# FFN gate and up products by Strassen's scheme, weight sums made by accumulating transfers

## The chip, the core and the metric

The kernel runs on one core of a Trainium2 chip, in one launch. The metric is the device time of the launch in microseconds. Engines: PE multiplies, ACT and DVE work elementwise, POOL helps and issues some of the transfers, SP issues the others.

## What is computed

A hybrid block (gated linear attention and a state space scan, then a gated FFN) on 1024 tokens of width 1024 with 256 context tokens, followed by two attention layers. The FFN is what the change touches:

```python
def swiglu(h, w_gate, w_up, w_down):
    return (jax.nn.silu(h @ w_gate) * (h @ w_up)) @ w_down

x_lat = x_lat + m_lat[2][:, None] * rms_norm(y_lat, norm_mix_post[layer])
f_lat = swiglu(modulate(rms_norm(x_lat, norm_ffn_pre[layer]), m_lat[3], m_lat[4]),
               w_gate[layer], w_up[layer], w_down[layer])
x_lat = x_lat + m_lat[5][:, None] * rms_norm(f_lat, norm_ffn_post[layer])
```

with `w_gate` and `w_up` of 1024 x 2816 and `w_down` of 2816 x 1024, in float32.

## The kernel before, in words

Activations lie with features on partitions and tokens along the free axis; "half" `ch` is one of two blocks of 512 tokens. Each float32 product is made of three products of a narrower type: every weight and every activation is split into a high half and a low half, and `pe_gemm` (L350) issues high x high, high x low and low x high for each block of 128 rows.

Weights go through one stream, class `Weights` (L251). A unit is up to 128 x 1024 elements per partition block: SP loads it into one of three `stage` slots (`sp_weights`, L302), ACT casts it to its high half `whi` (`act_weights`, L319), DVE subtracts to get the low half `wlo` (`dve_weights`, L332), PE uses both; there are four slots of halves. Each engine runs through its own program in order and calls its weight function two units ahead of the product it is at. All orders are written by hand.

The stages, with their places in the profile's time: modulation and projections; the scans (some 415 to 700 us: state space first, `pool_ssd` L1464, then gated linear attention, `pool_gla` L1917); the output product `wo` with the norms around it (`pe_out` L2312, `act_out`, `dve_out`, `pool_out` L2338; second token half from about 713 us); the FFN (`pe_ffn` L2377, `act_ffn`, `dve_ffn`, 764 to 1512 us); the two layers.

Small steps of norms, additions and splits run beside the products: class `Beside` (L2133) holds a list, and each `tick()` pops one step on every engine. `OUT1` holds the steps beside the second half of `wo`, `FFN0` and `FFN1` those beside the FFN of each token half. `Halves` (L2095) is the split of the FFN's input: for each 128 features one ACT step (add the shift, round to the high half) and one DVE step (low half). PE starts on the first 128 features once they are split.

FFN: the hidden width is cut in `PARTS` of 8, 8 and 6 blocks of 128. In a part, each block takes a gate product and an up product (24 matmuls of 512 columns each), ACT's Silu, DVE's multiplication, ACT's high half `uh` and DVE's low half `ul`; then eight down products add to the output `yc`.

POOL issues the loads of `x` (`xc`, one token half at a time, here from `pool_out` and `pool_moves` L2474) and stores. DVE's scale step of the post norm waits for the load of `x` together with the norm.

The functions that the diff touches, as the profile numbers them:

Of the kernel before, what the change touches and what calls it, by code (L numbers as in the profile page):

```python
# [4 lines left out]
ALU = mybir.AluOpType  # L5
# [10 lines left out]
NTB = 9  # L16
# [16 lines left out]

def down_units():
    return [(k, n, c, 128) for k, n in ((0, 8), (8, 8), (16, 6)) for c in range(0, 1024, 128)]
# [6 lines left out]
    "wg": fm(1024, 0, DFF),  # L42
    "wu": fm(1024, 0, DFF),
# [82 lines left out]
class Engine:  # L126
# [81 lines left out]
    def dma_start(self, out, in_):  # L208
        return IssuedDma(self.e and self.e.dma_start(out, in_))
# [41 lines left out]
class Weights:  # L251
# [4 lines left out]

    def __init__(self, S, H, L, land, hi, lo, aps):
        self.S, self.H, self.L, self.land, self.hi, self.lo, self.aps = S, H, L, land, hi, lo, aps
        self.seq, self.half, self.by, self.last, self.count = [], [], {}, {}, 0
        self.rows = None  # L260
        self.restart()
# [4 lines left out]
    def take(self, key, name, i, raw, count, *step):  # L266
        u = self.u
        self.u += 1
        if u == len(self.seq):
            self.seq.append((name, i, raw))  # L270
            self.half.append(self.count)
            self.count += not raw
# [3 lines left out]
        return u  # L276

# [4 lines left out]
    def staged(self, u):  # L282
        k, nk, c, n = self.shape(u)
        return self.S[:, u % self.NS, 0:nk * n]

    def halves(self, u):
        k, nk, c, n = self.shape(u)
        return [x[:, self.half[u] % self.NH, 0:nk * n] for x in (self.H, self.L)]
# [5 lines left out]
    def half_before(self, u):  # L294

        for v in range(u - 1, -1, -1):
            if not self.seq[v][2] and self.half[v] == self.half[u] - self.NH:
                return v
        return None


def sp_weights(e, W, upto):  # L302
    while W.sp_u <= min(upto, len(W.seq) - 1):
# [5 lines left out]
        if u >= W.NS:  # L309
            v = u - W.NS  # L310
            if W.seq[v][2]:
                e.wait_ge(*W.used(v))
            else:
                e.wait_ge(*W.lo[v])
        e.dma_start(W.staged(u), W.aps[name][off:off + 128 * nk * n].rearrange("(p x) -> p x", p=128)).then_inc(
            *W.land[u % W.NS].up(u, by=16))


def act_weights(e, W, upto):  # L319
    while W.hi_u <= min(upto, len(W.seq) - 1):  # L320
# [4 lines left out]
        e.wait_ge(*W.land[u % W.NS][u])  # L325
        v = W.half_before(u)
        if v is not None:
# [4 lines left out]
def dve_weights(e, W, upto):  # L332

    while W.lo_u <= min(upto, len(W.seq) - 1):
# [7 lines left out]
        v = W.half_before(u)  # L342
        if v is not None:
            e.wait_ge(*W.used(v))
        e.wait_ge(*W.land[u % W.NS][u])
# [4 lines left out]
def pe_gemm(e, W, bank, psum, key, name, units, rhs, nch, N, done, count, M=128, among=range(8), each=False, cuts=None):  # L350
# [5 lines left out]
    for n, i in enumerate(units):  # L356
# [5 lines left out]
        for ka, kb in zip(cuts or (0, nk), (cuts or (0, nk))[1:]):  # L362
            for ci, (b, free) in enumerate(bs):
# [19 lines left out]
                if n == len(units) - 1:  # L383
                    done.mark(key, ci)
                    if each and ci == nch - 1:
                        done.mark("row", key, nk - 1)

# [25 lines left out]
def mixer(K):  # L413
# [20 lines left out]
    stage = K.W.S[:, :, :].rearrange("p a b -> p (a b)")  # L434
# [168 lines left out]
    def dve_mod_row(e, m, D, ctx):  # L603
# [3 lines left out]
        e.wait_ge(*W.land[u % W.NS][u])  # L607
# [855 lines left out]

    def pool_ssd(e):  # L1464
# [667 lines left out]

class Beside:  # L2133
# [14 lines left out]
def blocks(K):  # L2148
# [30 lines left out]
    xc, nx, gg, sqf = v(3, 8, 512), (v(8, 8, 512), v(7, 8, 512)), v(8, 2, 512), v(8, 4, 512, off=1024)  # L2179
    yc = (v(1, 8, 512), v(2, 8, 512))  # L2180
    fh, fl, uh, ul = (v(i, 8, 512, dt=F32R) for i in (4, 0, 5, 6))
    w0 = v(1, 8, HT)
# [9 lines left out]
    def residual(key, st, ch, col, dst, sq4, ready, free, by_two=None):  # L2192
        n = Norm((key, ch), st, yc[ch], 512, aff[:, col, :], yc[ch], sq4, rs2[:, 0:512], ready, free=free, by_two=by_two)
# [14 lines left out]
    def last_of(st, key):  # L2208
# [3 lines left out]
                       [(sout.dve, ("lo", "f0", 7)), (sout.act, ("hi", "f0", 7))] if ch else [(K.sgla.pe, ("yo", 7))],  # L2212
                       (lambda k: [(sout.act, (("wo", 0, 2 * k + 1), 0))]) if ch == 0 else None) for ch in range(2)]
# [3 lines left out]
                  by_two=pair_of(sout, ("post", ch)), late=[(sout.act, ("sq", ("pre", ch), 3))])  # L2217
             for ch in range(2)]
    hf = [Halves(f"f{ch}", sout, fh, fl, nx[ch], lambda k, ch=ch: [(sout.dve, ("sc", ("pre", ch), k))],
                 [(sout.pe, (("wo", 0, 7), 0))] if ch == 0 else [(sffn.pe, (("wu", 0, 21), 0))],  # L2220
                 B=mod[:, 24:32]) for ch in range(2)]
    DOWN = [[(sffn.dve, (("wd", ch, 2, 7), 0))] for ch in range(2)]
    n_end0 = residual("end", sffn, 0, 4, xc, sqf, [*DOWN[0], (xld, ("r", 0))],
                      [(sout.pe, ("root", ("pre", 1), 0))])
# [1493 lines left out]
```

## Time and profile before

| | |
|---|---|
| median of three runs | 3363.24 us (3360.55 to 3364.39) |
| the profiled execution's own time | 3361.19 us |
| its span, first to last instruction | 3359.4 us |
| mean granted TensorE clock | 0.988 of full |
| PE, DVE, ACT, POOL busy | 97%, 49%, 39%, 8% of the span |
| bytes moved | 328 MB, 98 GB/s over the span |

Durations of matmuls overlap in the profile, so what one costs is read from the distance of starts. A window's DMA share is the mean busy share of the 16 DMA engines in it, and can stand slightly over 1 by rounding at its edges. A transfer's issue on an engine is short; its landing comes later.

### The profile page before, as it was taken

The page shows a single profiled execution, that of the slowest core. Times are in us where ns is not written, and L with a number is a line of the kernel's source. Part 1 is how long each engine was busy: PE and PEld are TensorE (multiplying, and loading weights), DVE is VectorE, ACT ScalarE, POOL GpSimd, SP SyncE. Part 2 cuts the span into 40 slices and gives each one's busy share as a digit, 9 for nine tenths or more (in the row PEclk, how much of TensorE's full clock was granted, in tenths as well). Part 3 has the DMA queues.
Part 4 walks back from the last instruction along what each step waited for, and adds up shares of the span by engine and source line. Part 5 has one row for each costly group of instructions (what it writes and reads, how often), then busy time and mean ns, then how long its engine had stood idle before and what let it go on. Part 6 is the DMA issues. An engine that isn't in the chain of part 4 may idle for free.

```text
span 3359.4 us, 43733 instructions
## 1 busy us (share of the span) xinstructions
PE 3256.7 (97%) x18179; PEld 2585.9 (77%) x18179; DVE 1660.1 (49%) x2404; ACT 1321.2 (39%) x2266; POOL 252.8 (8%) x302
## 2 busy tenths in 40 slices
PE   6899888899999999999999999999999999999999
PEld 6677656787878878889955579999999555688887
DVE  6767576554343443345454553444434545534433
ACT  4532455454232333234445543333334455423322
POOL 1000313400000000000120000000000300000001
PEclk8999989999999999999999999999999999999999
DMA  6545213133333334333200112442432001124323
GB/s 246 167 156 164 82 44 114 58 127 112 120 115 96 97 94 170 94 94 118 88 1 7 51 48 89 132 131 85 149 128 85 6 7 51 47 88 134 108 94 113
DMA packets 97749, 328.24 MB, mean 98 GB/s; under 512 B 11456, under 2 KB 12880, under 8 KB 96784
## 3 DMA queue, kind: packets, MB, share of 16 engines
q1 hardware_dynamic: 77120, 252.55, 23.5%
q0 software_dynamic: 18896, 68.63, 5.9%
q10 hardware_dynamic: 1536, 4.26, 0.3%
q8 instruction: 144, 2.36, 0.3%
q14 instruction: 53, 0.43, 0.0%
HBM read 299.19 MB, written 26.21 MB: 97 GB/s over the span
## 4 chain that ended last, share of the span: by engine, by line
PE 90%; DVE 5%; ACT 2%; DMA 1%; issue 1%; ACTq 0%; DVEq 0%; POOL 0%; POOLq 0%
PE psum L146 88%; DVE mixer L175 2%; PE psum L149 2%; DVE mixer L185 1%; DVE wlo L175 1%; DMA mixer<-in_wm 1%; DVE junk L189 1%; DMA stage<-in_wi 0%; ACT whi L163 0%; DMA hold<-in_wq 0%; ACT arena L154 0%; ACT mixer L154 0%; ACT mixer L155 0%; DVE mixer L180 0%; ACT mixer L163 0%
## 5 line engine op out<-in xcount | busy, mean ns | idle before, releaser
L146 PE MATMUL psum<-region,whi 128*128 128x260 f32 (+2 forms) x7616 | 1831.6, 333 | 1.8 <-DVE region L185 1.8
L146 PEld LDWEIGHTS psum<-region,whi 128*128 128x128 f32 (+1 forms) x7616 | 1279.7, 186 | 164.5 <-DVE region L185 3.1
L146 PE MATMUL psum<-region,wlo 128*128 128x260 f32 (+2 forms) x3808 | 1265.8, 332 | 0.0
L175 DVE TENSOR_TENSOR wlo<-stage,whi 128x1024 fp32r<-128x1024 f32 (+2 forms) x454 | 510.3, 1126 | 677.3 <-ACT whi L163 676.6
L146 PEld LDWEIGHTS psum<-region,wlo 128*128 128x128 f32 (+1 forms) x3808 | 711.2, 187 | 78.4
L163 ACT CAST whi<-stage 128x1024 fp32r<-128x1024 f32 (+2 forms) x454 | 432.2, 968 | 214.2 <-PE psum L146 173.4
L154 ACT ACTIVATE arena<-psum 128x512 f32<-128x512 f32 (+2 forms) x412 | 193.2, 469 | 775.1 <-PE psum L146 771.9
L146 PE MATMUL psum<-arena 128*128 128x512 f32 (+11 forms) x1072 | 382.6, 480 | 1.9 <-ACT arena L154 1.4
L163 ACT COPY arena<-psum 128x260 f32<-128x260 f32 (+9 forms) x345 | 151.5, 444 | 402.4 <-PE psum L146 395.5
L175 DVE TENSOR_TENSOR arena<-arena,psum 128x512 f32<-128x512 f32 (+1 forms) x220 | 125.7, 572 | 327.3 <-PE psum L146 326.9
L175 DVE TENSOR_TENSOR arena<-arena 128x512 f32<-128x512 f32 (+8 forms) x341 | 204.5, 617 | 152.6 <-ACT arena L154 146.3
L146 PEld LDWEIGHTS psum<-arena 128*128 128x128 f32 (+5 forms) x1072 | 166.8, 182 | 129.6 <-issue 102.7
L163 ACT CAST region<-arena 128x512 fp32r<-128x512 f32 (+3 forms) x202 | 120.4, 616 | 228.7 <-DVE arena L175 215.6
L146 PE MATMUL psum<-mixer 64*64 64x64 f32 (+8 forms) x1876 | 184.7, 292 | 23.1 <-DVE mixer L175 14.3
L198 DVE TENSOR_REDUCE arena<-psum 128x1 f32<-128x264 f32 (+8 forms) x225 | 107.1, 505 | 199.4 <-PE psum L146 199.4
L146 PEld LDWEIGHTS psum<-mixer 64*64 64x64 f32 (+3 forms) x1876 | 129.9, 168 | 82.7 <-issue 34.3
L175 DVE TENSOR_TENSOR region<-arena,region 128x512 fp32r<-128x512 f32 (+2 forms) x188 | 117.8, 646 | 56.2 <-ACT region L163 54.0
L146 PE MATMUL psum<-hold,arena 128*128 128x384 f32 (+1 forms) x432 | 142.5, 486 | 2.4 <-DMA hold<-in_wq 2.4
L146 PEld LDWEIGHTS psum<-hold,arena 128*128 128x128 f32 (+1 forms) x432 | 77.5, 180 | 68.7 <-issue 14.9
L175 DVE TENSOR_TENSOR mixer<-mixer 128x512 f32<-128x512 f32 (+3 forms) x104 | 102.8, 999 | 36.9 <-ACT mixer L154 18.4
L146 PE MATMUL psum<-hh,whi 128*128 128x512 f32 (+3 forms) x240 | 91.7, 382 | 19.3 <-DVE hl L175 8.4
L154 ACT ACTIVATE arena<-arena 128x1040 f32<-128x1040 f32 (+7 forms) x111 | 97.0, 882 | 29.5 <-DVE arena L175 27.2
(166 smaller groups left out, 2677.6 us busy)
## 6 DMA issues: line engine op xcount, KB each, us to landing
stage<-in_w SPq DMA_DIRECT2D x144, 512.0 KB, 3.4
stage<-in_wi SPq DMA_DIRECT2D x55, 512.0 KB, 4.4
stage<-in_wo SPq DMA_DIRECT2D x48, 512.0 KB, 3.5
stage<-in_wg SPq DMA_DIRECT2D x44, 512.0 KB, 3.5
stage<-in_wu SPq DMA_DIRECT2D x44, 512.0 KB, 3.5
stage<-in_wm SPq DMA_DIRECT2D x42, 512.0 KB, 3.6
stage<-in_wd SPq DMA_DIRECT2D x32, 512.0 KB, 3.5
arena<-xr_scratch POOLq DMA_DIRECT2D x5, 2080.0 KB, 9.4
```

Source lines behind the costliest of these rows:

```text
L146: return Issued(self, self.e and self.e.matmul(out, w, x, start=start, stop=stop, skip_group_check=True))
L149: return Issued(self, self.e and self.e.transpose(out, a, ident))
L154: return Issued(self, e and e.activation(out, a, func, scale=scale))
L163: return Issued(self, e and e.copy(out, a))
L175: return Issued(self, e and e.tensor_tensor(out, a, b, op))
L185: return Issued(self, e and e.scalar_tensor_tensor(out, a, s, b, op0, op1))
L189: return Issued(self, e and e.tensor_tensor_reduce(out=out, in0=a, in1=b, scale=1.0, scalar=0.0, op0=ALU.mult, op1=ALU.add, accum_out=total))
L198: return Issued(self, e and e.tensor_reduce(out, a, AX.X, op, negate=negate))
```

## The change

Two neighbouring blocks of 128 hidden columns, the two halves of the 1024 input features and the two halves of a token block form a 2 x 2 by 2 x 2 block product. It is computed with seven products of 512 features x 128 columns x 256 tokens instead of eight (`PRODUCTS`). With a11, a12, a22 and a21 the quarters of the input (the first index counts tokens), the products use a11, a12, a22 and the sums s1 to s4 of quarters, and weight blocks 11, 22, 21 and the sums T1 to T4 of blocks.

- Weights: units of gate and up are now quarters (128 x 512 per unit), the stream's slots may be taken in halves, and two more weight tensors `tg` and `tu` hold T1 to T4.
- `tg` and `tu` are scratch tensors in device memory. POOL issues eight plain copies of blocks of `wg` and `wu` into them at the start of the scans (`weight_copies`), six accumulating transfers at the end of `pool_ssd` (`weight_sums(e, 0)`, behind a wait for the copies) and four at the start of `pool_out` (`weight_sums(e, 1)`, behind a wait for the six). SP's first load from either waits for the last of these.
- Input: `Quarters` replaces `Halves`. ACT adds the shift to all eight pieces in place, then eleven steps make the sums on DVE and the high and low halves of seven operands.
- Results: of a group's four PSUM banks three hold two products in turn. ACT copies M1, M5 and M7 out, DVE forms C11 to C22 with additions of 256 columns. Gate and up of a pair then take the old path, 1024 wide.
- `PARTS` counts pairs: 4, 4, 3. Buffers in the arena are laid out anew; the load of the first tokens' residual and of the positions is moved in POOL's order.

```diff
+PRODUCTS = (("M1", "11", "a11", "a"), ("M5", "T1", "s1", "c"), ("M7", "T3", "s3", "d"), ("M6", "T2", "s2", "b"),
+            ("M3", "22", "s4", "c"), ("M2", "21", "a12", "a"), ("M4", "T4", "a22", "d"))
+KEPT = {"M1": "m1", "M5": "m5", "M7": "m7"}
+BLOCKS = {"11": (0, 0), "T1": (0, 1), "T3": (1, 1), "T2": (2, 1), "22": (2, 0), "21": (3, 0), "T4": (3, 1)}
+def pe_pair(e, W, bank, psum, key, name, j, h, done, A, leave, tick):
+    us = W.pair(key, name, j, done)
...
+        e.wait_ge(*h(x))
+        e.wait_ge(*W.hi[u])
+        e.wait_ge(*W.lo[u])
+        for k in range(kt):
+            e.matmul(o, wh[:, k, :], h.hi[x][:, k, :], b not in begun and k == 0, False)
+            e.matmul(o, wh[:, k, :], h.lo[x][:, k, :], False, False)
+            ins = e.matmul(o, wl[:, k, :], h.hi[x][:, k, :], False, k == kt - 1)
...
+    def weight_copies(e):
+        for name, t in (("wg", "tg"), ("wu", "tu")):
+            for to, of in ((0, 0), (1, 1), (2, 2), (3, 3)):
+                e.dma_start(block_of(t, to), block_of(name, of)).then_inc(*K.tcopy.up(t, to, by=16))
+    def weight_sums(e, step):
+        e.wait_ge(*(K.tsum[0]["tu", 3] if step else K.tcopy["tu", 3]))
+        for name, t in (("wg", "tg"), ("wu", "tu")):
+            for to, of, b in ((2, t, 0), (3, t, 0)) if step else ((0, name, 1), (1, name, 2), (3, name, 2)):
+                e.dma_start(block_of(t, to), block_of(of, b), accum_op=ALU.add).then_inc(*K.tsum[step].up(t, to, by=16))
...
         pool_intervals(e)
+        weight_copies(e)
...
+        weight_sums(e, 0)
         G.mark("end")
...
+class Quarters:
+    ACT_ORDER = ("a11", "a22", "a12", "s1", "s3", None, None, "s2", None, None, "s4")
+    DVE_ORDER = (("lo", "a11"), ("lo", "a22"), ("sum", "s1"), ("sum", "s3"), ("lo", "a12"), ("lo", "s1"), ("sum", "s2"),
+                 ("lo", "s3"), ("lo", "s2"), ("sum", "s4"), ("lo", "s4"))
...
     def pool_out(e, bs):
+        K.weight_sums(e, 1)
         e.wait_ge(*K.sgla.pe["turn", 7])
         e.dma_start(xc, XT[:, :, 0:512]).then_inc(*xld.up("x", 0, by=16))
...
-    PARTS = ((0, 8), (8, 8), (16, 6))
+    PARTS = ((0, 4), (4, 4), (8, 3))
...
+            K.W.need[t] = (K.tsum[1], ("tu", 3))
```

**Order on POOL, the end of the scans.** `mixer` and `hold` are SBUF buffers of the scans, `arena` that of the later stages, `y_scratch` a tensor in device memory. Before:

```order
L175 TENSOR_TENSOR mixer<-mixer,hold 128x512
L209 DMA y_scratch<-mixer 128x4x128 x4
L175 TENSOR_TENSOR mixer<-mixer 128x512 x11
...
L171 COPY mixer<-hold 64x2x4x64 x2
L209 DMA arena<-in_xT 128x8x512
```

Now:

```order
L182 TENSOR_TENSOR mixer<-mixer,hold 128x512
L218 DMA y_scratch<-mixer 128x4x128 x4
L217 DMA tg_scratch<-in_wg 352x2048 x3
L217 DMA tu_scratch<-in_wu 352x2048 x3
L182 TENSOR_TENSOR mixer<-mixer 128x512 x11
...
L178 COPY mixer<-hold 64x2x4x64 x2
L217 DMA tg_scratch<-tg_scratch 352x2048 x2
L217 DMA tu_scratch<-tu_scratch 352x2048 x2
L218 DMA arena<-in_xT 128x8x512
```

Six accumulating transfers stand between the last store of the first scan and the first operation of the second, four before the load of x.

**Order on DVE, the start of the FFN.** `region` holds the operands of products, `arena` the values they are made from. Before:

```order
L185 SCALAR_TENSOR_TENSOR region<-arena,mod,region 128x512
L185 SCALAR_TENSOR_TENSOR arena<-arena,aff 128x512
L185 SCALAR_TENSOR_TENSOR region<-arena,mod,region 128x512 x4
L175 TENSOR_TENSOR wlo<-stage,whi 128x1024 x2
L175 TENSOR_TENSOR arena<-arena,psum 128x512
L175 TENSOR_TENSOR region<-arena,region 128x512
```

Now:

```order
L192 SCALAR_TENSOR_TENSOR arena<-arena,aff 128x512 x4
L182 TENSOR_TENSOR region<-arena,region 128x1024 x2
L182 TENSOR_TENSOR arena<-arena 128x4x256 x2
L182 TENSOR_TENSOR region<-arena,region 128x1024 x2
L182 TENSOR_TENSOR arena<-arena 128x4x256
L182 TENSOR_TENSOR region<-arena,region 128x1024 x2
L182 TENSOR_TENSOR arena<-arena 128x4x256
L182 TENSOR_TENSOR region<-arena,region 128x1024
L182 TENSOR_TENSOR wlo<-stage,whi 128x512 x3
L182 TENSOR_TENSOR arena<-arena,psum 128x256
```

Eight splits of 512, each right behind its scale, became eleven operations of 1024 elements behind all eight scales; weights' low halves follow in units of 512.

## Rows read from the trace of the kernel before

**Rows 1.** The page: span, busy time of each engine, and the chain that ended last.

```profile
span 3359.4 us, 43733 instructions
...
PE 3256.7 (97%) x18179; PEld 2585.9 (77%) x18179; DVE 1660.1 (49%) x2404; ACT 1321.2 (39%) x2266; POOL 252.8 (8%) x302
...
PE 90%; DVE 5%; ACT 2%; DMA 1%; issue 1%; ACTq 0%; DVEq 0%; POOL 0%; POOLq 0%
```

**Rows 2.** Busy times by window (us; last: granted clock, DMA share, GB/s), the FFN's first half.

```profile
core 0: us, PE busy (x) PEld busy (x) DVE busy (x) ACT busy (x) POOL busy (x), PEclk, DMA share, GB/s
...
764.00:1137.00 373.00, 371.47 (x1583) 296.01 (x1584) 159.03 (x191) 121.63 (x153) 3.23 (x4) 1.00 0.34 109
```

**Rows 3.** Groups of PE instructions by shape in the FFN, 764 to 1512 us.

```profile
L146 PE MATMUL psum<-region,whi 128*128 128x512 f32 x2112 | 665.5, 396 | 1.8 <-DVE region L185 1.8
L146 PE MATMUL psum<-region,wlo 128*128 128x512 f32 x1056 | 417.1, 395 | 0.0
```

**Rows 4.** Timeline of PE, 512 columns (start, duration, instruction).

```profile
899.63 0.40 PE L146 MATMUL psum<-region,wlo 128*128 128x512 f32 x1
...
904.54 0.39 PE L146 MATMUL psum<-region,wlo 128*128 128x512 f32 x1
```

**Rows 5.** Timeline of PE, 260 columns.

```profile
1659.76 0.28 PE L146 MATMUL psum<-region,wlo 128*128 128x260 f32 x1
...
1663.67 0.28 PE L146 MATMUL psum<-region,wlo 128*32 128x260 f32 x1
```

**Rows 6.** Timeline of DVE beside the output product, second half of the tokens.

```profile
721.92 0.75 DVE L185 SCALAR_TENSOR_TENSOR arena<-arena,aff 128x512 f32<-128x512 f32 x1 [4.16 <-ACT arena L154]
722.71 0.69 DVE L175 TENSOR_TENSOR arena<-arena 128x512 f32<-128x512 f32 x1
723.32 1.22 DVE L175 TENSOR_TENSOR wlo<-stage,whi 128x1024 fp32r<-128x1024 f32 x1
724.45 0.75 DVE L185 SCALAR_TENSOR_TENSOR arena<-arena,aff 128x512 f32<-128x512 f32 x1
```

**Rows 7.** Busy times by window: the densest stretch, then the stretches of the new transfers.

```profile
10.00:30.00 20.00, 9.76 (x47) 9.66 (x47) 14.68 (x23) 5.00 (x6) 0.71 (x1) 1.00 1.03 397
415.00:558.00 143.00, 122.94 (x669) 76.10 (x668) 104.59 (x181) 77.55 (x191) 17.25 (x16) 0.90 0.19 63
558.00:640.00 82.00, 79.06 (x1297) 63.66 (x1298) 41.21 (x59) 46.77 (x94) 59.05 (x43) 1.00 0.19 67
640.00:700.00 60.00, 54.31 (x344) 43.59 (x345) 26.55 (x53) 29.88 (x91) 2.13 (x3) 0.94 0.33 106
700.00:722.00 22.00, 22.00 (x96) 17.43 (x95) 8.61 (x9) 12.45 (x16) 1.82 (x2) 1.00 0.56 194
722.00:764.00 42.00, 41.54 (x196) 33.74 (x195) 27.17 (x33) 18.78 (x24) 0.85 (x1) 1.00 0.42 138
```

**Rows 8.** Timeline of PE at the start of the FFN.

```profile
763.90 0.71 PE L146 MATMUL psum<-region,whi 128*128 128x512 f32 x2 [0.46 <-DVE region L185]
...
771.07 0.39 PE L146 MATMUL psum<-region,wlo 128*128 128x512 f32 x1
```

**Rows 9.** Timeline of ACT at the start of the FFN.

```profile
762.17 3.17 ACT L155 ACTIVATE region<-arena,mod 128x512 fp32r<-128x512 f32 x5
```

**Rows 10.** Timeline of POOL from the scans to the output product.

```profile
413.59 0.58 POOL L209 DMA_DIRECT2D i_scratch<-mixer  x1 [0.30 <-POOL mixer L175]
...
558.09 0.75 POOL L209 DMA_DIRECT2D y_scratch<-mixer  x1 [2.18 <-ACT mixer L163]
560.46 1.78 POOL L175 TENSOR_TENSOR mixer<-mixer 128x512 f32<-128x512 f32 x1 [1.62 <-issue]
...
643.96 1.28 POOL L171 COPY mixer<-hold 64x512 f32<-64x512 f32 x2 [3.04 <-DVE hold L202]
702.04 0.94 POOL L209 DMA_DIRECT2D arena<-in_xT  x1 [56.81 <-PE psum L149]
```

**Rows 11.** Timeline of PE beside rows 6: the first matmul of the next weight unit.

```profile
718.82 0.80 PE L146 MATMUL psum<-y_hi,whi 128*128 128x512 f32 x1
```

More of the change, by code:

```diff
@@ L264, in restart, with align, place, take @@
         self.u = self.hi_u = self.lo_u = self.sp_u = 0
-    def take(self, key, name, i, raw, count, *step):
+    def align(self, spot, half):
+        self.next = [spot, half]
+    def place(self, which, own, size, width, u):
+        at = self.next[which] + (width == 2 and self.next[which] % 2)
+        at = 0 if at + width > size else at
+        self.next[which] = at + width
+        before = sorted({v for v in own[at:at + width] if v is not None})
+        own[at:at + width] = [u] * width
+        return at, before
+    def take(self, key, name, i, raw, count, *step, width=2):
         u = self.u
@@ L276, in take, with pair @@
         return u
+    def pair(self, key, name, j, done):
+        t = "t" + name[1]
+        us = {}
+        for b, (n, kind) in BLOCKS.items():
+            us[b] = self.take((key, b), (name, t)[kind], 11 * n + j, False, done, "unit", self.u, width=1)
+        self.pairs[key] = us
+        return us
     def shape(self, u):
@@ L292, in used, with landed, room @@
         return count[step]
[L294 to L299, printed above, removed]
+    def landed(self, u):
+        return self.land[self.spot[u]][u]
+    def room(self, u):
+        out = [self.used(v) if self.seq[v][2] else self.lo[v] for v in self.sprev[u]]
+        if self.seq[u][0] in self.need:
+            count, step = self.need[self.seq[u][0]]
+            out.append(count[step])
+        return out
 def sp_weights(e, W, upto):
@@ L324, in act_weights @@
             continue
-        e.wait_ge(*W.land[u % W.NS][u])
-        v = W.half_before(u)
-        if v is not None:
+        e.wait_ge(*W.landed(u))
+        for v in W.hprev[u]:
             e.wait_ge(*W.used(v))
@@ new lines, in act_shift, with act_quarter @@
+def act_shift(e, h, k):
+    for c, s in h.ready(k):
+        e.wait_ge(*c[s])
+    e.activation(h.src[:, k], h.src[:, k], ACT.Identity, bias=h.B[:, k:k + 1], own=False).then_inc(
+        *h.st.act.up("shift", h.key, k))
+def act_quarter(e, h, i):
+    A, D, x = h.st.act, h.st.dve, h.ACT_ORDER[i]
+    if x is None:
+        return
+    e.wait_ge(*A["shift", h.key, 7 if x != "a11" else 3])
+    if i == 0:
+        for c, s in h.free:
+            e.wait_ge(*c[s])
+    if x in h.sums:
+        e.wait_ge(*D["sum", h.key, x])
+    e.copy(h.hi[x], h.at[x], own=False).then_inc(*A.up("hi", h.key, x))
@@ new lines, in dve_quarter @@
+def dve_quarter(e, h, i):
+    A, D = h.st.act, h.st.dve
+    what, x = h.DVE_ORDER[i]
+    e.wait_ge(*A["shift", h.key, 7 if i else 3])
+    if what == "lo":
+        if i == 0:
+            for c, s in h.free:
+                e.wait_ge(*c[s])
+        e.wait_ge(*A["hi", h.key, x])
+        e.tensor_tensor(h.lo[x], h.at[x], h.hi[x].bitcast(F32), ALU.subtract, own=False).then_inc(*D.up("lo", h.key, x))
+    else:
+        out, a, b, op = h.sums[x]
+        e.wait_ge(*A["hi", h.key, {"s1": "a22", "s3": "a11", "s2": "a11", "s4": "a12"}[x]])
+        for y in {"s2": ("s1",), "s4": ("s2",)}.get(x, ()):
+            e.wait_ge(*D["sum", h.key, y])
+        e.tensor_tensor(out, a, b, op, own=False).then_inc(*D.up("sum", h.key, x))
@@ L2424, in act_ffn @@
                 key = ("wd", ch, part, m)
-                act_weights(e, W, W.last[key] + 2)
+                act_weights(e, W, ahead_down(key, m))
                 if part == 0:
                     e.wait_ge(*T[key, 0])
-                    e.copy(yc[ch][:, m], psum[:, bank.of[key, 0], :], own=False).then_inc(*A.up(key, 0))
-                bs.tick(2 if part == 2 else 1)
+                    e.wait_ge(*(sffn.dve["add", ("end", 0), m] if ch else sout.dve["add", ("post", 1), m]))
+                    e.copy(yd[:, m], psum[:, bank.of[key, 0], :], own=False).then_inc(*A.up(key, 0))
```

334 lines of the change are left out of this document (230 added, 104 removed).

## The prediction

> **What bounds the kernel now.** I read the page first: PE is busy 97% of the 3359.4 us span, and 90% of the chain that ended last is PE's [rows 1]. A change helps if it takes columns away from PE and leaves nobody else late. Then the windows of the FFN: in its first half PE is busy 371.5 of 373 us, DVE 159, ACT 122, at a granted clock of 1.00 (the 2.4 GHz level), with the DMA engines a third busy [rows 2]. The reader should see that nothing but PE's own work limits this stretch. The groups by shape then give its size: 2112 + 1056 matmuls of 512 columns [rows 3]. Of these 22 x 2 x 2 x 8 x 3 = 2112 are gate and up, 1056 are down.
>
> What one costs is read from starts in the timeline, since durations overlap: 21 matmuls of 512 columns from 899.63 to 904.54 are 233.8 ns each [rows 4]; 33 of 260 columns from 1659.76 to 1663.67 are 118.5 ns each [rows 5]. Per column that is 0.457 and 0.456 ns: a narrow matmul pays no fixed price. So 256 columns cost 116.7 ns.
>
> **The products.** For a pair of 128-column weight blocks and one name, 2 x 2 x 2 half-width products become seven: 7 x 4 x 3 = 84 matmuls of 256 instead of 48 of 512. There are 11 x 2 x 2 = 44 such groups, so 3696 x 0.1167 = 431.3 us replace 2112 x 0.2338 = 493.8 us: **-62 us**, all on PE's path.
>
> **The load on DVE and ACT.** From starts in the timeline of DVE a 512-wide DVE operation takes 0.61 us and a 1024-wide one 1.13 [rows 6]; by the line through both, 256 take 0.34 and 768 take 0.87. One pair of blocks (gate and up) gives DVE 14 low halves (8.5), eleven operations of 256 (3.7), one of 768 (0.87) and one of 1024 (1.13): 14.2 us, while PE takes 168 x 0.1167 = 19.6. That is 72%, where it was about 6.9 of 22.4. Norm work of the other token half rides along in the first seven pairs: some 24 us in 137, another 17%. 90% is tight, but PE sees DVE only through the low halves, made five products (7 us) ahead. I cost it at nothing; the cover is those 7 us. ACT comes to some 11 us of 19.6. SP loads 14 x 256 KB per 19.6 us, 187 GB/s, against 397 GB/s in the densest stretch [rows 7], with six half slots: nothing.
>
> **The start of the FFN.** Before, each of eight pieces was scaled, halved and used at once: first product at 763.90, last of its 24 matmuls at 771.07 [rows 8], so ended 771.3, 1.8 us more than 24 x 0.234. Now eight shifts come first on ACT (0.5 us each, from the 3.17 us of five that overlap [rows 9]), from 762.2 to 766.4, then a11's high half to 767.4. DVE then does eleven 1024-wide steps in a row, 12.4 us, to 780; the product M3 needs the last. M3, M2 and M4 take 1.4 us each after it, to 784, where undisturbed seven would end at 763.9 + 9.8 = 773.7. That is 10.5 late, less the old 1.8: **+9 us** (6 to 13; the upper end takes in a granted clock at the 1.2 GHz level while PE has gaps). For the second token half the same steps stand beside the last down products and cost nothing.
>
> **Ends of parts.** After the last product of a part DVE needs 0.34 + 0.34 + 0.87, ACT 0.97, DVE 1.13, with hand-offs 4.3 us. PE reaches the last pair's rows after 18 x 0.234 = 4.2 us in parts of four pairs, after 12 x 0.234 = 2.8 in the part of three. Two times 1.5 and some tenths: **+3 us**.
>
> **The transfers.** A block is 11 x 512 x 128 x 4 bytes = 2.88 MB. POOL issues eight copies (23.1 MB) after 413.6, six accumulating ones (17.3 MB) after 558.8, four more (11.5 MB) ahead of the x load that stood at 702.0 [rows 10].
> - The copies have until 558. At 397 GB/s they need 58 us of the 116 that are free there (143 us at a share of 0.19 [rows 7]): hidden, also at half that rate.
> - The six issues stand ahead of the operation at 560.46 [rows 10]; an issue takes 0.75 us, so it is 4.5 us late, on a chain in which POOL, ACT and PE alternate: **+3 us** (0 to 5).
> - No row shows an accumulating transfer. Bounds from the densest stretch: at least as cheap as a plain one (397 GB/s), or at half (198), since it reads its destination too. Below, a third (132), if reads and write share one path. Free DMA time [rows 7]: 66 us in 558 to 640, 40 in 640 to 700, 15 in 700 to 722 and 30 in 722 to 764 (the x load and a store, 5.3 us each, now stand behind and are taken out). At 397 the six end at 612 and the four, issued at 645, at 689: no delay. At 198 the six (87 us) end at 673, the four (58 us) at 757, and the x load, which is queued behind them on POOL, lands at 765. Queued behind that wait on DVE is everything: the scale at 721.92 reads x, and the low half at 723.32, which the fourth output unit needs, stands behind it [rows 6]. PE has two more units (718.82 + 2 x 5.6 = 730.0 [rows 11]) and the low half comes 2.5 us after x: the delay is landing minus 727.5, here 37 us. At 132 the four end at 832, the x load at 838: 110 us.
>
> The densest stretch is all loads into SBUF that read once; the accumulating transfer differs by one read. I take the middle of no delay and 37: **+18 us**, and keep 0 and 110.
>
> The Trainium skill ("Collectives: The Full Stack", the bandwidth ceiling) holds that a reducing transfer runs at half a copy's rate because both sources go through the same read ring. By that the term would be 37, not 18. No row here shows it.
>
> **Sum.** -62 + 9 + 3 + 3 + 18 = -29 us. From the profiled execution, 3361.2 us, that is 3332; the median of the three runs is 3363.2, so against it the change is about 0.9%. I say **3333 us**.
>
> **Rivals.**
> - *The sums are late by far.* A wait on x on DVE takes the place of PE's work. It decides above a delay of 47 us, that is, if the x load lands after 774, at an accumulating rate under some 185 GB/s. At 132: -62 + 9 + 3 + 3 + 110 = +63, **3424 us**. For it: the two passes depend on each other, and the window is full. Against: 151 us of free DMA time for 28.8 MB.
>  A rule makes this likelier. "DMA: Bandwidth & Descriptors" of the Trainium skill (latency and other measured facts) gives full-rate copies between two HBM tensors as 207 to 214 GB/s. By that a plain copy is already at half of 397, an accumulating one at about a third, and the time is this rival's. The trace holds no large HBM to HBM transfer, so nothing here confirms or denies it.
> - *Fully hidden.* Accumulating costs no more than copying. -62 + 9 + 3 + 3 = -47, **3314 us**. For it: free time; against: the second read.
> - *DVE becomes the bound in the FFN.* If hand-offs add 0.1 us to each of its 27 operations per pair, 90% becomes over 100% for seven pairs, and PE's lead of 7 us is used up: some 20 us more, **3350 us** with the 18.
> - *It doesn't do what it says*, if narrow products cost as much as wide ones: the 260-column products [rows 5] exclude it.
>
> **How the numbers follow.** The forecast (delay 0 to 37, which takes in the fully hidden case) has 0.55, the late sums 0.33, a bound DVE or a worse start 0.12. The forecast alone spans 3310 to 3356. To leave out no more than two in ten the range must reach into the late sums: **3308 to 3425**. A measurement of this kernel tells 0.2% (7 us) from nothing. Faster: 0.52 of the forecast and 0.06 of the DVE case, 0.58; within 0.2%: 0.05; slower: 0.32 of late sums and 0.05 of the rest, 0.37.
>
> **What would show it.** In the new profile: 256-column matmuls 117 ns apart; gate and up about 62 us shorter; FFN products M5 to M3 each waiting on DVE's low halves once, at the first pair. DVE's scale at the post norm either follows the root within 4 us (hidden) or waits for a DMA; the length of that wait is the term I know least. I am wrong in mechanism if POOL stands still in the scans waiting for the copies (landing after 558), if SP's weight loads are late beside the sums, or if PE waits for low halves throughout the FFN.

## The result, and where the time went

| | median | range | ratio to before, 95% |
|---|---|---|---|
| before, run beside it | 3361.89 us | 3358.51 to 3364.39, 4 runs | |
| the change | 3418.61 us | 3416.86 to 3420.59, 4 runs | 1.017 (1.0152 to 1.0187) |

The change is 57 us slower; I had forecast 28 us faster than the profiled run of the kernel before. The profiled execution took 3416.86 us, its span 3415.1, 55.7 more than in [rows 1]. From the page of the changed kernel:

```profile
PE 3209.9 (94%) x19763; PEld 2633.3 (77%) x19763; DVE 1833.4 (54%) x2828; ACT 1452.8 (43%) x2610; POOL 264.6 (8%) x320
...
PE 82%; DVE 7%; ACT 3%; DMA 3%; another core or an unknown queue 2%; issue 1%; ACTq 0%; DVEq 0%; POOL 0%; SPq 0%; POOLq 0%
```

PE has less work, as wanted, but its share of the chain fell from 90% to 82%. The first question is where. POOL's timeline answers it, since it has a mark at the end of each stage; the columns are start, duration, instruction, and the wait ahead of it:

```profile
415.57 2.04 POOL L218 DMA_DIRECT2D tg_scratch<-in_wg  x4
417.60 1.97 POOL L218 DMA_DIRECT2D tu_scratch<-in_wu  x4
...
596.61 0.75 POOL L218 DMA_DIRECT2D y_scratch<-mixer  x1 [2.19 <-ACT mixer L170]
597.35 3.02 POOL L217 DMA_DIRECT2D tg_scratch<-in_wg  x3
599.20 4.03 POOL L217 DMA_DIRECT2D tu_scratch<-in_wu  x3
...
695.24 1.92 POOL L217 DMA_DIRECT2D tg_scratch<-tg_scratch  x2 [4.32 <-DMA tu_scratch<-in_wu]
696.42 2.66 POOL L217 DMA_DIRECT2D tu_scratch<-tu_scratch  x2
778.75 0.96 POOL L218 DMA_DIRECT2D arena<-in_xT  x1 [79.67 <-PE psum L156]
```

Against [rows 10]: the copies start at the same time; the last y store is 38.5 us late (596.61 for 558.09); the last copy of the second scan, at 689.64 for 643.96, is 45.7 late; the x load, at 778.75 for 702.04, is 76.7 late. So 38.5 us went in the first scan, 7.2 in the second, 31.0 ahead of the output's end. In the FFN 25.4 us come back (a root product, the matmuls with which PE adds up the squares of a norm, stands behind the FFN at 1567.27 for 1515.94, 51.3 late), and the layers lose 4.4 in two small steps near 1850 and 2600, which I did not follow. 38.5 + 7.2 + 31.0 - 25.4 + 4.4 = 55.7.

The first of these is the least exact. The profiles of e1 and e5 below hold the same instructions up to the end of the scans, and yet the last store ahead of the first scan stands at 411.74 and 414.90, the last y store at 549.83 and 559.37: two executions differ by 10 us up to here, 6 of them in the first scan alone.

The windows of the same stretches, to be laid beside [rows 7]:

```profile
core 0: us, PE busy (x) PEld busy (x) DVE busy (x) ACT busy (x) POOL busy (x), PEclk, DMA share, GB/s
415.00:500.00 85.00, 38.83 (x180) 24.45 (x180) 32.35 (x54) 23.87 (x43) 7.41 (x11) 0.68 0.93 316
500.00:558.00 58.00, 53.04 (x279) 31.43 (x280) 45.89 (x72) 35.08 (x95) 7.37 (x6) 0.94 0.10 28
558.00:640.00 82.00, 67.65 (x777) 51.10 (x779) 42.39 (x81) 42.45 (x98) 37.96 (x31) 0.96 0.68 185
640.00:700.00 60.00, 51.59 (x836) 40.80 (x832) 33.70 (x54) 32.97 (x85) 37.80 (x31) 0.96 0.98 207
...
722.00:764.00 42.00, 14.16 (x73) 11.41 (x71) 4.83 (x8) 7.84 (x25) 0.00 (x0) 0.67 1.02 245
```

In the first and last of these PE is busy under half of the time and the DMA engines nearly all of it, most of it with blocks that PE needs only in the FFN. The waits in 415 to 770 (total, times, longest) say what PE lacked:

```profile
ACT whi L170 <- DMA stage<-in_wo: 42.6, 2, 40.0
...
PE psum L153 <- DVE mixer L192: 33.7, 6, 29.3
...
DVE mixer L192 <- DMA g_scratch<-stage: 30.6, 1, 30.6
PE psum L153 <- DVE wlo L182: 27.8, 1, 27.8
...
ACT stage L162 <- DMA g_scratch<-stage: 10.3, 1, 10.3
```

None of these is a wait for the new transfers. DVE's 30.6 and ACT's 10.3 wait for SP's 256 KB stores of gates, ACT's 40.0 for one of SP's 512 KB loads of output weights: small transfers that the kernel had always made, now queued beside large ones. PE's 29.3 and 27.8 wait for what DVE makes behind them. The list of DMA issues in 415 to 500, and under it the two lines on g_scratch of the kernel before in the same window (KB each, median us to landing):

```profile
tg_scratch<-in_wg POOLq DMA_DIRECT2D x4, 2816.0 KB, 25.4
tu_scratch<-in_wu POOLq DMA_DIRECT2D x4, 2816.0 KB, 60.2
g_scratch<-mixer SPq DMA_DIRECT2D x4, 256.0 KB, 33.4
g_scratch<-stage SPq DMA_DIRECT2D x4, 256.0 KB, 27.3
```

```profile
g_scratch<-mixer SPq DMA_DIRECT2D x4, 256.0 KB, 2.4
g_scratch<-stage SPq DMA_DIRECT2D x4, 256.0 KB, 2.7
```

**In the FFN.** 256-column matmuls stand 117.9 ns apart (33 of them from 859.19 to 863.08), so 3696 take 435.8 us where the wide ones took 493.8: -58. But PE waits in two new places. These are its waits from 860 to 1600:

```profile
PE psum L153 <- DVE arena L182: 15.3, 4, 5.7
PE psum L153 <- DVE region L182: 3.2, 3, 1.4
```

The three `region` waits are the ends of parts. The four `arena` waits are root products of norms that ride along: steps beside the products are popped every 3.3 us where it was 5.6, and DVE's sum is not ready when PE's next step comes. DVE is itself nearly full there. In the 12 us up to the first of these roots (883.73) it is busy 94%, in the 12 us up to the second (1233.48) 93%; this is the window ahead of the first:

```profile
872.00:884.00 12.00, 7.17 (x60) 6.99 (x59) 11.24 (x18) 7.67 (x12) 0.00 (x0) 0.95 0.52 156
```

### The profile page after: what moved, and what is told of

Read it like the earlier page. It is cut to its first block, busy times and chain, and to the rows that moved or that the text cites. A ratio compares the mean times of both kernels' runs of the same rounds, so it can differ in the third digit from the quotient of the medians.

```text
span 3415.1 us, 48462 instructions
## 1 busy us (share of the span) xinstructions
PE 3209.9 (94%) x19763; PEld 2633.3 (77%) x19763; DVE 1833.4 (54%) x2828; ACT 1452.8 (43%) x2610; POOL 264.6 (8%) x320
## 4 chain that ended last, share of the span: by engine, by line
PE 82%; DVE 7%; ACT 3%; DMA 3%; another core or an unknown queue 2%; issue 1%; ACTq 0%; DVEq 0%; POOL 0%; SPq 0%; POOLq 0%
PE psum L153 81%; DVE mixer L182 2%; PE psum L156 1%; DVE mixer L192 1%; DVE wlo L182 1%; DVE arena L182 1%; ACT whi L170 1%; DMA hold<-i_scratch 1%; DMA mixer<-in_wm 1%; DVE region L182 1%; DMA g_scratch<-stage 1%; ACT arena L161 1%; DVE junk L196 1%; DMA stage<-in_wi 0%
## 5 line engine op out<-in xcount | busy, mean ns | idle before, releaser
L153 PEld LDWEIGHTS psum<-region,whi 128*128 128x128 f32 x8672 | 1396.2, 187 | 113.7 <-DVE region L182 14.1
L182 DVE TENSOR_TENSOR wlo<-stage,whi 128x512 fp32r<-128x512 f32 (+2 forms) x674 | 609.8, 912 | 650.6 <-ACT whi L170 645.9
L153 PEld LDWEIGHTS psum<-region,wlo 128*128 128x128 f32 x4336 | 813.6, 188 | 46.3
L170 ACT CAST whi<-stage 128x512 fp32r<-128x512 f32 (+2 forms) x674 | 520.4, 799 | 256.6 <-PE psum L153 165.3
L161 ACT ACTIVATE arena<-psum 128x512 f32<-128x512 f32 (+4 forms) x390 | 175.3, 450 | 653.7 <-PE psum L153 650.5
L170 ACT COPY arena<-psum 128x256 f32<-128x256 f32 (+7 forms) x477 | 200.6, 424 | 506.9 <-PE psum L153 499.9
L182 DVE TENSOR_TENSOR arena<-arena 128x256 f32<-128x256 f32 (+10 forms) x459 | 271.5, 605 | 153.9 <-ACT arena L161 144.4
L182 DVE TENSOR_TENSOR arena<-arena,psum 128x260 f32<-128x260 f32 (+2 forms) x242 | 122.8, 508 | 213.4 <-PE psum L153 213.0
L170 ACT CAST region<-arena 128x520 fp32r<-128x520 f32 (+4 forms) x194 | 130.5, 695 | 79.2 <-DVE arena L182 66.1
L182 DVE TENSOR_TENSOR region<-arena,region 128x520 fp32r<-128x520 f32 (+3 forms) x180 | 130.9, 749 | 38.9 <-ACT region L170 36.7
```

Of the source, the lines that this page charges most:

```text
L153: return Issued(self, self.e and self.e.matmul(out, w, x, start=start, stop=stop, skip_group_check=True))
L161: return Issued(self, e and e.activation(out, a, func, scale=scale))
L170: return Issued(self, e and e.copy(out, a))
L182: return Issued(self, e and e.tensor_tensor(out, a, b, op))
```

## The experiments

Before is 3358.91 to 3362.83 us in the medians that were run beside them. Where only one run was made, no interval is given.

**e1: no transfers at all.** The seven products read blocks of `wg` and `wu` that are not summed; copies and sums are left out, in e5 too.

```diff
-            K.W.aps[t] = nc.dram_tensor(f"{t}_scratch", ...).ap()
-            K.W.need[t] = (K.tsum[1], ("tu", 3))
+            K.W.aps[t] = I["w" + t[1]]
-        weight_copies(e)
-        weight_sums(e, 0)
-        K.weight_sums(e, 1)
```

> The changed kernel without any of the eighteen transfers: SP loads the blocks of wg and wu in the place of their sums, so the FFN computes with unsummed blocks. Both theories of the transfers (A: POOL's long rows hold up SP's short transfers; B: the DMA engines are simply full) expect the fillers ahead of the FFN back at 747 us, where the changed kernel had them at 824. The FFN then shows what it is worth by itself: the changed profile ran it in 743 us from fillers to the next root where the kernel before took 769, so 3336 to 3341 us. My recorded sum without the transfers was 3361 - 47 = 3314. If it comes out near 3314, the FFN of the changed profile was itself slowed by the transfers; near 3338, the terms for the FFN were mis-sized.

3339.64 us (3335.94 to 3341.30), ratio 0.994 (0.9923 to 0.9956), as expected. The scheme in the FFN is worth 21 us, the -25.4 + 4.4 of the changed kernel. All else, some 79 us, comes with the transfers. The root waits are there too, 14.9 us:

```profile
PE psum L153 <- DVE arena L182: 14.9, 4, 5.3
```

**e2: copies, no sums.** The sums are left out; SP's loads of T blocks wait for the copies.

```diff
-            K.W.need[t] = (K.tsum[1], ("tu", 3))
+            K.W.need[t] = (K.tcopy, ("tu", 3))
-        weight_sums(e, 0)
-        K.weight_sums(e, 1)
```

> Only the eight plain copies; the ten accumulating transfers are left out, so the FFN computes with copies in the place of sums. If the first 38 us of delay (last y_scratch store at 596.6 instead of 558.1) belong to the copies alone, this kernel shows the same store at 596 +- 2, no further delay behind it, and a time 37 to 40 us above the kernel without transfers, some 3377. If the accumulating transfers caused more than the 7 and 31 us that the profile shows behind that store, it is lower.

3382.68 us in one run, 43 over e1, where 37 to 40 were expected; the last y store stands at 599.49, and behind it the second scan and the output lose nothing (85.9 us to POOL's last copy and 58.8 from there to the x load, 85.9 and 58.1 before). Plain copies that nobody waits for cost as much as all sums together, or more (3418.61 - 3382.68 = 36); the stores of g_scratch take 33.4 and 27.4 us.

**e4: rows of 2 KB in all transfers.**

```diff
-            ... accum_op=accum_op, max_dma_last_dim=8192
+            ... accum_op=accum_op, max_dma_last_dim=2048
-                e.dma_start(block_of(t, to), block_of(name, of))      # copies
+                e.dma_short(block_of(t, to), block_of(name, of))      # max_dma_last_dim=2048
```

> All eighteen transfers, same bytes, same places, but in rows of 2 KB (1408 x 512) where copies had 64 rows of 45 KB and sums 352 rows of 8 KB. A (a DMA engine takes turns between queues row by row, so a long row of POOL's holds up SP's short ones): the last y_scratch store comes before 570 us, the g_scratch stores land in under 10 us, and the total falls below 3385. B (full engines, whatever the rows): the store stays at 594 to 598 and the total at 3413 to 3423, or above, since short rows carry more overhead.

3436.33 us in one run, 18 over the change, so the total lies on B's side (3413 to 3423, or above). Yet the last y store is only 14 us late (571.92) where it was 38.5, and g_scratch lands in 9.7 and 14.2 us: near the marks that A had set (570 and 10) and far from B's 594 to 598. The trace counts 4.0 KB to a packet of the copies here (22.97 MB in 5645, 415 to 500 us), 35 KB in the change. Beside the last four sums the output loses nothing: 58.1 us from POOL's last copy to the x load, as before. What made it slow is a third thing, in POOL's timeline:

```profile
572.82 4.64 POOL L220 DMA_DIRECT2D tg_scratch<-in_wg  x3
575.50 4.99 POOL L220 DMA_DIRECT2D tu_scratch<-in_wu  x2
651.82 1.49 POOL L220 DMA_DIRECT2D tu_scratch<-in_wu  x1 [71.33 <-issue]
```

POOL could issue five accumulating transfers of 1408 rows and stood still for 71 us in front of the sixth; the second scan, which needs POOL, stood with it (PE busy 17.4 of the 82 us from 558 to 640). The profile names no releaser for this wait. The eight short copies had gone out in 7 us (416.55 to 423.46).

**e5: e1 with two empty steps ahead of three roots.**

```diff
-        return n, n.steps() + ...
+        return n, n.steps(0, 2, 0) + ...
-    FFN0 = ... n_pre[1].steps() + ...
+    FFN0 = ... n_pre[1].steps(0, 2, 0) + ...
-    FFN1 = ... n_in[0].steps(6, 0, 0)
+    FFN1 = ... n_in[0].steps(6, 2, 0)
```

> As without transfers, and with two empty steps ahead of the root of the norms that run beside the FFN and layer start. The beside steps come every 3.3 us now instead of every 5.6, and PE waited 4.8, 5.7, 3.2 and 1.6 us for DVE's sum at a root. If that is the cause, the waits fall under 1 us each and the kernel is 9 to 15 us faster than without the gaps (some 3326). Rival: DVE is late throughout (85% busy), then later steps wait instead and the gain is under 3 us.

3335.18 us (3332.27 to 3337.36), ratio 0.9924 (0.9909 to 0.9939): 4.5 under e1, between what the theory (9 to 15) and the rival (under 3) gave. The waits only fell to 11.5 us in five places, up to 3.9 us each, not to under 1. So the shorter lead is not shown to be the whole cause, and a DVE that is busy over 90% ahead of the roots stays a second one; a longer lead was not tried.

**e7: the copies moved to SP, behind the weight loads of the projections.**

```diff
+    def copy_piece(self, e):        # 44 pieces of 512 KB, rows of 4 KB
+        ...
+            e.dma_start(out, in_).then_inc(...)
 def sp_weights(e, W, upto):
...
+        if name == "wi":
+            W.copy_piece(e)
-        weight_copies(e)
```

> Only the copies are moved: SP issues them as 44 pieces of 512 KB with rows of 4 KB, each right behind one weight load of the projections (about 100 to 350 us), where the share of the DMA engines was 0.4 to 0.5. POOL's sums stay where the change has them. Theory (the first scan lost 38 us because eight copies were queued at once beside SP's small stores): the first scan is as in the kernel before, last store of y at about 558, and the whole is 38 us shorter than the change, 3380, plus what 44 copies on SP's own queue cost the projections (1.8 us each, hidden: 0 to 8 us). Since the six sums start 38 us earlier relative to the FFN's start nothing changes in the losses of the second scan (7 us) and of the output (31 us). Rival (the amount of bytes is what costs, wherever it is moved): the projections lose 30 us or more and the time stays within 10 us of 3418.

3378.82 us in one run: 40 under the change, as forecast, with the last y store at 555.47. The same 23 MB cost nothing there. Three things changed at once (the place, the queue, and rows of 4 KB instead of 45), so e7 doesn't say which of them frees the first scan. The DMA share from 100 to 300 us is 0.70 where it was 0.475, PE is as busy as before (184.5 of 200 us for 183.9):

```profile
100.00:200.00 100.00, 87.37 (x351) 65.92 (x352) 74.17 (x99) 44.41 (x59) 0.00 (x0) 0.97 0.72 247
200.00:300.00 100.00, 97.11 (x415) 75.95 (x413) 64.98 (x84) 33.85 (x51) 4.89 (x9) 1.00 0.68 234
```

The loss ahead of the FFN stays (ACT's wait for in_wo 39.8, PE's behind it 27.7).

**e6: e7, and the sums issued one by one within the scans.** POOL issues the six in steps 0 to 5 of the first scan, the four in steps 2, 10, 18 and 26 of the second.

```diff
+            for at, r_ in enumerate((0, 1, 2, 3, 4, 5)):      # pool_ssd
+                if r_ == r:
+                    some_sums(e, 0, at)
+            for at, r_ in enumerate((2, 10, 18, 26)):         # pool_gla
+                if r_ == r:
+                    some_sums(e, 1, at)
```

> Copies as in e7; besides, POOL issues the six sums one by one in steps 0 to 5 of the first scan (from about 446 to 520), and the four others one by one in steps 2, 10, 18 and 26 of the second scan, so that they have landed before the output projection. Theory (queued transfers starve the loads of other queues only where those are on the path; the output projection, fed by 512 KB weight loads, lost 31 us to it): the loss of 31 us ahead of the FFN goes, 3380 - 31 = 3349, and some 5 to 15 us of it may come back as small waits on stores and loads within the scans: 3345 to 3365. Rival (accumulating transfers cost the same wherever they lie): 3375 to 3390, with waits on DMA in the scans of 30 us or more in all.

3365.21 us (3362.01 to 3370.97), ratio 1.0015 (1.0005 to 1.0024), at the upper end of the theory's range. What is left lies in the first scan, where four sums met the stores of g_scratch: the last y store stands at 580.35, 22.3 late, and PE waits 24.7 us once. The second scan and the output lose 1 us together. The wait for such a store in 415 to 560:

```profile
ACT stage L162 <- DMA g_scratch<-stage: 22.9, 1, 22.9
```

**e8: three sums at the end of the projections, three late in the first scan; e9: e8 with e5's gaps.**

```diff
+                        if ring == 8:          # pool_proj
+                            some_sums(e, 0, 0); some_sums(e, 0, 1)
+                        if ring == 12:
+                            some_sums(e, 0, 2)
+            if r in (5, 7, 9):                 # pool_ssd
+                some_sums(e, 0, 3 + (r - 5) // 2)
```

> As e6, but no sum stands beside the eight stores of g_scratch (about 415 to 475) any more: three of the six first sums are issued by POOL at the end of the projections (from about 345, when the copies have landed, to 366), the other three in steps 5, 7 and 9 of the first scan (about 507 to 550), the four last in steps 4, 11, 18 and 25 of the second scan. In e6 the whole loss of the first scan, 24 us, came from its sums beside those stores (waits of 22.9 on g_scratch and 24.7 behind it), and the second scan and the output lost nothing. Theory (what costs is only a transfer queued beside a load or store that is on the path): 20 of the 24 us go, 3365 - 20 = 3345, at best e1's 3340, at worst 3352. Rival (the sums merely find the next thing to delay, here the last loads of the projections, the z and r stores and the z loads): 3358 to 3370, with DMA waits of 15 us or more between 340 and 640.

> e8 with the gaps of e5 (two empty steps ahead of the root of each norm that rides along in the FFN). In e5 the gaps were worth 4.4 us on top of e1. If the two effects lie in different stages they add: 4 us (2 to 6) under e8, 3341; if e8's theory fails the difference of 4 stays all the same.

3368.75 us (3361.76 to 3372.97), ratio 1.0024 (1.0014 to 1.0033), and 3365.44 us (3362.86 to 3367.88), ratio 1.0012 (1.0002 to 1.0021). The rival was right for these places: two sums at 311 met the projections' last weight loads, and the third of the late ones, at 560, a y store. The gaps are worth 3.3 us here, within the spread of both. The waits in 330 to 760 of e8:

```profile
ACT whi L170 <- DMA stage<-in_wi: 18.6, 4, 13.2
ACT mixer L170 <- DMA y_scratch<-mixer: 12.4, 1, 12.4
```

**e10: every sum where nothing wanted stands beside it; copies as in e7, gaps as in e5.**

```diff
+                        if ring == 12:         # pool_proj, behind the last r store
+                            some_sums(e, 0, 0)
+        some_sums(e, 0, 1)                     # pool_ssd, behind the load of the masks
+            if r in (3, 5, 7):                 # pool_ssd
+                some_sums(e, 0, 2 + (r - 3) // 2)
+            if r == 2:                         # pool_gla; then 9, 15, 21, 27
+                some_sums(e, 0, 5)
```

> Copies as in e7, gaps as in e5, and each sum in a place where nothing on the path moves: sum 0 behind the last r store of the projections (366), sum 1 behind the load of the level masks (391), sums 2 to 4 in steps 3, 5 and 7 of the first scan (about 485 to 530), sum 5 in step 2 of the second scan, the four last in its steps 9, 15, 21 and 27. e8 lost 18.6 us to two sums issued at 311 beside the last loads of the projections' weights and 12 us to the sum at 560 beside the y store; its sums at 385, 516 and 539 and all four of the second scan cost nothing. Theory (only the neighbours count): the two losses go, 3365 - 30 = 3335, which is e5, 3335; with small remains 3335 to 3346. Rival (each place has a neighbour; five sums in a row in the second scan land after the output's weight loads begin): 3350 to 3362.

3338.58 us (3333.02 to 3345.40, 6 runs) against 3358.91 (11 runs), ratio 0.9939 (0.9927 to 0.9951): 20 us faster than before and 80 faster than the change, with all its arithmetic and all its bytes; some 4 of the 80 belong to the gaps. Two windows of e10:

```profile
415.00:500.00 85.00, 75.18 (x364) 44.30 (x366) 61.79 (x98) 50.19 (x114) 11.89 (x9) 0.91 0.40 101
...
558.00:640.00 82.00, 76.94 (x1321) 61.24 (x1319) 44.89 (x62) 45.63 (x96) 59.81 (x45) 1.00 0.99 225
```

In the second the DMA engines have a share of 0.99 throughout, and PE is busy 76.9 of 82 us, where it was 79.1 at a share of about 0.2. DMA engines that are full throughout cost some 2 us here.

**e11, e12, e13: e10 with the last four sums back in the output projection, in three ways.** e11 issues them in one row, e12 one at a time, e13 in one row with rows of 2 KB.

```diff
     def pool_out(e, bs):
+        for at in range(4):                            # e11, e13
+            K.some_sums(e, 1, at)
+        K.some_sums(e, 1, 0)                           # e12
+        e.wait_ge(*W.hi[W.last["wo", 0, 4]])
+        K.some_sums(e, 1, 1)
+        e.wait_ge(*W.hi[W.last["wo", 0, 7]])
+        K.some_sums(e, 1, 2)
+        ...                                            # x load
+        e.wait_ge(*W.hi[W.last["wo", 1, 2]])
+        K.some_sums(e, 1, 3)
```

> As e10, but the four last sums are issued in one row ahead of the x load, at about 641, as the change does at 695. Theory (a row of sums starves whatever SP loads next): the output's 512 KB weight loads take up to 40 us again, PE stands still 25 to 35 us in the output projection, 3339 + 25 to 35 = 3364 to 3374. Rival (the change lost those 31 us only because the six sums before them were late as well): 3339 to 3348.

> The same bytes in the same stage as e11, but one sum at a time: at 641, then behind the high halves of output units 4 and 7 (about 675 and 690), the last behind the x load and the high half of unit 10 (about 712, landed by 728, before the first load of a summed block at 734). If the backlog of several sums starves the loads: 3340 to 3350, loads of in_wo at most 10 to 15 us. If any sum beside the output's weight loads costs its time: 3360 to 3375 as e11.

> e11 with one edit: the four last sums, still issued in one row at about 644, have rows of 2 KB instead of 8 KB. In e11, 655 to 698, the two queues' packets were 1022 and 1023, so they take turns packet by packet, and SP gets 1.95 MB in 43 us, 45 GB/s, where the output projection wants 512 KB per 5.6 us, 94 GB/s. Theory (turns by packet, so the share of SP's loads goes with the length of the other queue's packets): with packets a quarter as long PE does not stand still for in_wo; the 23 us that e11 lost to e10 go, less what the x load is late behind longer transfers (up to 10 us): 3339 to 3350. Rival (the backlog of four transfers starves SP whatever their rows): 3360 to 3372.

| | median us (range) | ratio, 95% | before beside it |
|---|---|---|---|
| e11, one row | 3362.10 (3355.87 to 3366.23) | 1.0004 (0.9995 to 1.0014) | 3360.75 |
| e12, paced | 3337.69 (3333.35 to 3347.84) | 0.9927 (0.9911 to 0.9944) | 3360.75 |
| e13, one row, 2 KB | 3342.46 (3336.59 to 3346.89) | 0.9935 (0.9918 to 0.9952) | 3362.83 |

e11 lies 2 us under its theory's range and far over its rival's; e12 lies 2 us under the range for the case that only the backlog costs; e13 lies in its theory's range. The same bytes in the same stage cost 24 us in one row, nothing paced, and 4 in short rows, against e10's 3338.58. Waits of e11 in 620 to 800:

```profile
ACT whi L170 <- DMA stage<-in_wo: 40.2, 2, 38.9
...
PE psum L153 <- DVE wlo L182: 26.8, 1, 26.8
```

Why, is in the packets of the two queues (packets, MB, share). First the changed kernel from 443 to 475, then e11 from 655 to 698, then e13 in that window; q0 is POOL's, q1 SP's:

```profile
q0 software_dynamic: 290, 10.18, 93.8%
q1 hardware_dynamic: 289, 0.53, 4.4%
```

```profile
q0 software_dynamic: 1022, 7.98, 89.3%
q1 hardware_dynamic: 1023, 1.95, 13.8%
```

```profile
q0 software_dynamic: 2951, 5.98, 75.5%
q1 hardware_dynamic: 1897, 5.10, 33.9%
```

Where both queues always have work they take turns packet by packet: 290 to 289, 1022 to 1023. A turn of SP's is 1.8 to 1.9 KB; a turn of POOL's is 35 KB in the copies and 7.8 KB in the sums (bytes over packets). So SP gets 0.53 MB in 32 us, 17 GB/s, beside the copies, and 1.95 MB in 43 us, 45 GB/s, beside the sums, where the output projection wants 512 KB in 5.6 us, 94 GB/s. In e13 a packet of POOL's is 2.0 KB, SP gets 119 GB/s, and PE's longest wait for weights in the stage is 1.7 us. In e12 SP's share is low while a sum runs: the loads of in_wo take 10.6 us where e10, without sums in the stage, needs 3.5 (median to landing, the first line e10's, the second e12's). But a sum is over after some 20 us, and the weights that are loaded ahead cover that; four in a row are nearly 60 us.

```profile
stage<-in_wo SPq DMA_DIRECT2D x13, 512.0 KB, 3.5
...
stage<-in_wo SPq DMA_DIRECT2D x12, 512.0 KB, 10.6
```

The Trainium skill ("DMA: Bandwidth & Descriptors", Queues, rings and completion order) states this rule: each DMA engine goes round between the queues that have work, one packet at a time. By that rule a queue's share depends on the other's packet size, and these counts agree with it. I had not weighed it.

e13 isn't free: its four transfers of 1408 rows are slower (70.7 us median to landing for the later pair, 56.5 in e11), and the x load queued behind them on POOL is late, a DVE wait of 13.9 us on it. That is the wait that I had forecast for the change.

## Why the prediction was wrong, step by step

- **The range.** 3418.6 lies inside the 3308 to 3425 that I gave. That is no merit: the range reached up there only for the case of late sums on the x load, which did not happen. The forecast itself said faster, and the kernel is slower.
- **Products, -62.** Right: -58.
- **DVE and ACT in the FFN, nothing.** Right for the low halves of the products: PE does not wait for them once. Wrong for what rides along: the cover of 7 us that I named belongs to the low halves, and a root product has no such lead. 15.3 us. My estimate of a DVE 90% busy was about right ahead of the first two roots (94% and 93%); that it costs nothing was not.
- **Start of the FFN, +9.** 823.93 to the end of the seventh product at 863.1 is 39.2 us, for 24.1 from 747.21 to 771.3 before; 4.2 more of it is work that the groups have anyway. That leaves +10.9, for 9 and in the range of 6 to 13, with PE at the 1.2 GHz level for the first products (846.21 on, starts 214 ns apart).
- **Ends of parts, +3.** Three waits, 3.2 us.
- Together the FFN gives -28.6 by these numbers and -25.4 in the trace. The 3 us between them I put down to the clock, which stands at 0.53 of full from 884 to 890 behind such a wait (the two matmuls of a root then take 2.05 us, 1.10 before); that is argued, not tested.
- **"At 397 GB/s they need 58 us of the 116 that are free there (...): hidden, also at half that rate."** This is the step that failed: it put the copies at nothing. The rate was fine: POOL's queue moved 318 GB/s from 443 to 475, all eight copies were in by about 494, and nobody waited for them. What I took for free time of the engines was time in which small transfers on the path need to be served at once. The step priced the new transfer's own landing and not what it does to the landing of others: 38.5 us in the profile, 43 in e2, 40 in e7.
- **SP's weight loads, nothing.** The same fault. I checked them for bandwidth in the FFN, against the densest stretch, and never beside the sums: 31.0 us in the output projection.
- **Six issues, +3.** The second scan lost 7.2, of which 4.7 are PE's wait for the load of `hold<-i_scratch`, again a small load beside sums.
- **The x load, +18.** DVE never waited for it: the starved weight loads had made its stage so late that the sums were in when it was issued at 778.75, and it landed 8.7 us later. The rate was near my middle bound, 186 GB/s (e11, 655 to 698) for 198, for which I had a delay of 37 and took half. The sums' whole cost, 7.2 + 31.0 = 38.2, comes close to that 37, but another transfer paid.
- **Rivals.** The time of the late sums, 3424, is near the measured one, and its mechanism isn't: no wait on x, and half of the loss lies in the copies, which it priced at nothing. DVE did not become the bound of the FFN as a whole, only ahead of the roots. e1's 3340 stands where I had 3314 for fully hidden; 15 of the 26 us between them are the roots.
- I had named "SP's weight loads are late beside the sums" as a sign that I was wrong in mechanism. It was the right thing to look for, and it should have been a rival with a price.

## What to carry to other kernels

Here a background transfer was paid for not in bandwidth but in what it did to the latency of the transfers beside it. Before adding one, list the loads and stores on the path in its window, and compare the packet sizes of the two queues. Against e11, three cures were worth 20 to 24 us: put the transfer where nothing wanted is queued (e10, 24), keep one in flight at a time so that the buffers' lead covers it (e12, 24), or cut its rows to the size of its neighbours' (e13, 20). The last has its price: in e4 the engine that issued the short rows stood still for 71 us. And steps that ride along with a faster loop come due sooner: when the loop gets shorter, check their lead again, and how full the engine is that makes them.

## What the runs showed of the hardware that was not expected

- Two DMA queues that both have work share the DMA engines by turns of a packet: 290 and 289 packets in 32 us, with 35 KB a packet on one side and 1.8 KB on the other. A 256 KB store that took 2.4 us before took 33.4.
- Copies from device memory to device memory moved 318 GB/s on one queue at a share of 93.8% of the 16 engines (the change, 443 to 475). The Trainium skill ("DMA: Bandwidth & Descriptors", Latency and other measured facts) gives 207 to 214 GB/s for copies between HBM tensors at full rate, in tiles of 128 x 16 KiB on the sync and scalar queues. The transfers here have another form, and for them the measurement decides.
- Accumulating transfers moved 186 GB/s at a share of 89.3% (e11, 655 to 698). Per share that is 208 to 339, 0.61 of a copy. The Trainium skill ("Collectives: The Full Stack", the bandwidth ceiling) gives a half for a reducing against a copying transfer; the trace is nearer to that than to no difference.
- POOL, issuing accumulating transfers of 1408 rows of 2 KB, stood still for 71.33 us in front of the sixth (e4). Six of 352 rows of 8 KB it issued in 6 us (the change, 597.35 to 603.23).
- DMA engines busy at a share of 0.99 for 82 us left PE busy 76.9 of them (e10, 558 to 640), where it was 79.1 at a share of 0.19. At a share of 0.93 beside SP's small stores it was busy 38.8 of 85 (the change, 415 to 500), where it was 73.4.
